# A two-layer decoder trunk: the first gain row spread by TensorE, the turn between layers summed by transfers, and transposes moved behind gate tiles

## The reference

```python
xn = rmsnorm(h, pre_g[i])
y = mixer_i(xn)                     # xn @ w_in, mixing over tokens, then @ w_out
h = h + rmsnorm(y, post_g[i])
gate = sigmoid(rmsnorm(h, ple_g[i]) @ w_ple_gate[i])
h = h + gate * (p[i] @ w_ple[i])
# rmsnorm: x * rsqrt(mean(x*x) + EPS) * g, one mean per token
```

## Time and profile before

| what | value |
|---|---|
| median of 3 runs | 1005.5 us (1005.45 to 1008.51) |
| the profiled execution, time | 1008.02 us |
| its span, first to last instruction | 1006.2 us |
| PE busy | 978.7 us (97%) |
| DVE busy | 642.7 us (64%) |
| ACT busy | 507.4 us (50%) |
| POOL busy | 91.7 us (9%) |
| moved by transfers | 150.37 MB, mean 149 GB/s |

### The profile page before, as it was taken

How to read it: one execution, slowest core, us unless ns; L and a number is a source line. 1 busy time by engine, 2 the same in 40 slices (tenths; PEclk the granted TensorE clock), 3 DMA queues, 4 the chain that set the end, 5 groups by cost and what they waited for, 6 DMA issues and landing times.

```text
span 1006.2 us, 12025 instructions
## 1 busy us (share of the span) xinstructions
PE 978.7 (97%) x4486; PEld 803.1 (80%) x4486; DVE 642.7 (64%) x863; ACT 507.4 (50%) x832; POOL 91.7 (9%) x148
## 2 busy tenths in 40 slices
PE   6999999999999999998989999999999999999998
PEld 4888888888877888786778888888888888888776
DVE  5767788786874225658886856776576676421835
ACT  6454545555562233546546647465654775341722
POOL 2020110100000003103000011010101000000500
PEclk9999999999999999999989999999999999999999
DMA  9555946848361523422938465573839063242122
GB/s 360 184 147 147 276 140 171 213 164 209 65 207 42 216 84 105 168 84 87 229 145 209 125 168 138 155 180 113 222 124 239 12 170 135 92 160 84 45 81 84
DMA packets 24760, 150.37 MB, mean 149 GB/s; under 512 B 3072, under 2 KB 4224, under 8 KB 8448
## 3 DMA queue, kind: packets, MB, share of 16 engines
q1 hardware_dynamic: 18800, 106.63, 27.7%
q0 software_dynamic: 5904, 42.99, 22.1%
HBM read 145.42 MB, written 4.19 MB: 149 GB/s over the span
## 4 chain that ended last, share of the span: by engine, by line
PE 88%; DVE 5%; ACT 3%; issue 2%; POOL 2%; DMA 1%; POOLq 0%; DVEq 0%; ACTq 0%
PE bank L2035 17%; PE bank L2038 16%; PE bank L2037 16%; PE bank L1962 8%; PE bank L1963 8%; PE bank L1964 8%; PE bank L2059 2%; PE bank L2060 1%; PE bank L2061 1%; PE bank L2288 1%; DVE w_lo L1309 1%; ACT square L683 1%; PE bank L2270 1%; PE bank L2292 1%; DMA raw<-in_slots 1%
## 5 line engine op out<-in xcount | busy, mean ns | idle before, releaser
L1309 DVE TENSOR_TENSOR w_lo<-raw,w_hi 128x1024 fp32r<-128x1024 f32 x204 | 240.8, 1222 | 140.0 <-ACT w_hi L719 136.4
L2035 PE MATMUL bank<-w_hi,l_hi 128*128 128x512 f32 x784 | 318.2, 406 | 6.8 <-issue 4.3
L2038 PE MATMUL bank<-w_hi,l_lo 128*128 128x512 f32 x784 | 306.9, 392 | 0.0
L2037 PE MATMUL bank<-w_lo,l_hi 128*128 128x512 f32 x784 | 306.6, 391 | 0.0
L719 ACT ACTIVATE w_hi<-raw 128x1024 fp32r<-128x1024 f32 x204 | 204.4, 1053 | 84.7 <-PE bank L2038 50.6
L2035 PEld LDWEIGHTS bank<-w_hi,l_hi 128*128 128x128 f32 x784 | 148.0, 189 | 40.8 <-issue 10.3
L2038 PEld LDWEIGHTS bank<-w_hi,l_lo 128*128 128x128 f32 x784 | 147.9, 189 | 31.6
L2037 PEld LDWEIGHTS bank<-w_lo,l_hi 128*128 128x128 f32 x784 | 148.1, 189 | 30.3 <-issue 1.0
L1274 DVE TENSOR_TENSOR w_lo<-raw,w_hi 128x1024 fp32r<-128x1024 f32 x52 | 61.3, 1222 | 117.3 <-ACT w_hi L672 117.2
L672 ACT ACTIVATE w_hi<-raw 128x1024 fp32r<-128x1024 f32 x52 | 52.3, 1057 | 134.2 <-PE bank L1964 122.3
L1962 PE MATMUL bank<-w_hi,y_hi 128*128 128x512 f32 x224 | 90.6, 404 | 0.2 <-DVE y_lo_end L1487 0.2
(11 more groups left out here) (221 smaller groups left out, 1190.2 us busy)
## 6 DMA issues: line engine op xcount, KB each, us to landing
raw<-in_slots SPq DMA_DIRECT2D x86, 1024.0 KB, 6.5
raw<-in_slots POOLq DMA_DIRECT2D x41, 1024.0 KB, 8.4
h<-in_x SPq DMA_DIRECT2D x8, 512.0 KB, 5.9
out<-h SPq DMA_DIRECT2D x4, 512.0 KB, 4.3
h<-out SPq DMA_DIRECT2D x4, 512.0 KB, 7.0
out<-h SPq DMA_DIRECT2D x8, 256.0 KB, 2.0
p_sb<-in_p SPq DMA_DIRECT2D x2, 512.0 KB, 3.8
g_post<-in_g_rows SPq DMA_DIRECT2D x2, 512.0 KB, 5.7
```

The lines of the kernel that those rows point to most:

```text
L1309: dve.tensor_tensor(w7_lo[:, ring(g), c], raw7[:, source(*STEPS[g]), c], w7_hi[:, ring(g), c].bitcast(F32), ALU.subtract).then_inc(w7_lo_r ...
L2035: pe.matmul(dst[:, :], left_hi, w7_hi[:, r, c], start=(first and k == 0), stop=False, skip_group_check=True)
L2037: pe.matmul(dst[:, :], left_hi, w7_lo[:, r, c], start=False, stop=False, skip_group_check=True)
L2038: done = pe.matmul(dst[:, :], left_lo, w7_hi[:, r, c], start=False, stop=(k == 3), skip_group_check=True)
```

## The change

Four things are changed.

**Start.** The gain row goes to one partition, and PE spreads it over the others with two matmuls against a row of ones; DVE copies the result out of PSUM. Unit 0's first block arrives in two halves, each with its semaphore, and is split half by half, with the left operand's parts in between. The two wide warming matmuls become 11 and 6 small ones.

**Norms.** ACT's squares are scaled so that they sum to the mean, and POOL's `rstd_of` has two operations instead of three, in all 24 norms of this kind.

**Tails.** The last tile's transposes (`transpose_x(l, 3)`) follow the gate's first token tile in both layers. The second layer's first transposes (`first_transpose(1, 0)`) follow the whole gate.

**Turn.** Unit 7's sums of weights are made by four adding transfers (into BV, twice into BX, into BA) in place of DVE's four half-block additions and one adding transfer; B12 is loaded twice for it. Buffer names change with it, for unit 7 and the even units behind it. ACT, DVE and POOL have another order of work from the second half of the gate to the end of unit 7.

```diff
 def x_buffer(u):
-    return BX if u % 2 else BV
+    return BX if u % 2 else BV if u < LEAD else BA
+def a_buffer(u):
+    return BA if u < LEAD else BV
+def s6_count(u):
+    return 2 * (u - (u >= LEAD))
...
+        sp.dma_start(scaled[0:1, 1], g_rows[0:1, :]).then_inc(g_in, 16)
         sp.dma_start(h[:, 0], x[0:P, :]).then_inc(x_in[0], 16)
-        row(g_first, g_rows[0:1, :], g_in)
         sp.dma_start(h[:, 1], x[P:2 * P, :]).then_inc(x_in[1], 16)
-        block_in(0, B11, BX, x_raw_in)
+        for half in range(2):
+            c = slice(half * SLOT // 2, (half + 1) * SLOT // 2)
+            sp.dma_start(raw7[:, BX, c], slots[B11][:, c]).then_inc(w_first[half], 16)
...
-        block_in(FIRST[1], B12, BV, v_raw_in)
+        block_in(FIRST[1], B12, BV, a_in)
...
         sp.wait_ge(gated_ready, 8)
+        block_in(FIRST[1], B12, BA, v_raw_in)
         for t in range(TILES):
             sp.dma_start(out[t * P:(t + 1) * P, :], h[:, t]).then_inc(h_out, 16)
...
             pool.wait_ge(ready, count)
-            link(pool.tensor_tensor(dst, first, second, ALU.add))
-            link(pool.tensor_scalar(dst, dst, 1.0 / D, EPS, ALU.mult, ALU.add))
+            link(pool.tensor_scalar(dst, first, second, EPS, ALU.add, ALU.add))
...
         tail_norms(0)
+        pool.wait_ge(a_in, 16 * LEAD)
+        add_in(LEAD, B11, BV, added_in[5])
+        pool.wait_ge(w7_lo_ready, split_done(LEAD, 1))
+        add_in(LEAD, B12, BX, s6_added)
         for t in range(TILES):
             pre(4 + t)
+        pool.wait_ge(s6_added, 16)
+        add_in(LEAD, B22, BX, s6_added)
...
-        pool.wait_ge(s5_sum, 2)
-        add_in(FIRST[1], B22, BV, added_in[7])
+        pool.wait_ge(v_raw_in, 32)
+        add_in(LEAD, B22, BA, added_in[7])
...
@@ ACT, start
-        hi7(0)
-        first_left(0)
+        first_high(0)
+        first_left(0, (0,))
+        first_high(1)
+        first_left(0, (1,))
+        first_left(1)
         x_squares(2)
-        first_left(1)
         first_full(0)
@@ ACT, gate of layer 0
+            tanh(1, 3)
             if l == 0:
                 left(1, 0, 0, 1, 11)
+                next_norm(2, 1)
                 left(1, 0, 1, 2, 12)
-            tanh(1, 3)
-            if l == 0:
-                next_norm(2, 1)
+                next_norm(3, 1)
                 left(1, 1, 0, 1, 11)
                 left(1, 1, 1, 2, 12)
-                next_norm(3, 1)
                 hi7(TURN + 1)
+                left(1, 2, 0, None, 21)
+                left(1, 2, 1, 4, None)
+                b_copy(LEAD, 0)
+                left(1, 3, 0, None, 21)
+                left(1, 3, 1, 4, None)
+                b_copy(LEAD, 1)
@@ DVE, unit 7, all of it after the change
+        left_7(1)
+        left_sum(1, 5)
+        lo7(TURN + 2)
+        left_6(1)
+        lo7(TURN + 3)
+        left_sum(1, 6)
+        left_3(1)
+        left_sum(1, 7)
+        left_sum(1, 3)
+        lo7(TURN + 4)
+        lo7(TURN + 5)
+        c_make(7, 0)
+        c_make(7, 1)
+        lo7(TURN + 6)
+        gate_rows()
+        lo7(TURN + 7)
+        s5_make(7, 0)
+        s5_make(7, 1)
+        gate_sums()
+        lo7(TURN + 8)
+        s6_add(8)
+        gate_maxima(0)
+        gate_maxima(1)
@@ PE, start
+        for half in range(2):
+            pe.matmul(bank[half][:, :], mask[0:1, :], scaled[0:1, 1, half * SEQ:(half + 1) * SEQ], start=True,
+                      stop=True).then_inc(g_spread, 1)
+        warming(11)
         first_transpose(0, 0)
-        for tp in range(2):
-            done = pe.matmul(b_of(tp)[:, :], ident[:, :], h[:, 0, 0:SEQ], start=True, stop=True)
-        done.then_inc(warm, 1)
+        warming(6).then_inc(warm, 1)
@@ PE, tail
-            transpose_x(l, 3)
...
-                        if l == 0 and nb == 1 and q == 1 and t == 2:
-                            first_transpose(1, 0)
+                        if q == 0 and nb == 0 and t == 0:
+                            transpose_x(l, 3)
...
         tail(0)
+        first_transpose(1, 0)
         first_transpose(1, 1)
         product(7, 1, 0)
```

160 lines of the change are left out of this document (72 added, 88 removed).

## The result

The changed kernel takes 995.95 us (median of 4 runs, 995.63 to 996.68) where the kernel before takes 1005.88 (4 runs, 1005.45 to 1008.51); the ratio is 0.9898, with an interval of 0.9883 to 0.9914. The forecast was 991.7, so the direction was right and the measured time 4.2 us above it: outside the forecast's own range (989.5 to 993), inside the outer one (988.5 to 996.5). The profiled execution took 995.63 us (span 993.6), against 1008.02 for that of before: 12.4 us between the profiles, 9.9 between the medians. The sum was made against the profile, so it is compared with the profile: 16.3 promised, 12.4 delivered.

What follows compares the result with a forecast made beforehand. PE, 97% busy, was taken as the bound, losing time only at four places. Start 1.75, first tail 4.0, turn 7.95, second tail 2.6 sum to 16.3: 1008.0 - 16.3 = 991.7 us; range 989.5 to 993, outer 988.5 to 996.5.

Steps and rivals of the forecast that it cites:

- the four places: Start, first tail, turn and second tail hold what PE lacks; all the rest is PE at its pace, untouched.
- Start: Kernel start: first block lands earlier, first product at 12.3, product 21 near 20; 1.75 us saved, bounds 0.5 and 2.6.
- the small warming: Rival at the start: low clock in first products, or halves landing together; 1.25 us lost, 993.0; chance 0.06.
- 0.4 us in each tail: Both tails: one norm operation less on POOL shortens PE's wait for `gated` by 0.3 to 0.4 us, taken as 0.4.
- Transposes behind the gate's first tile: Both tails: the gate's first tile fills the 1.84 us wait; 3.6 us saved in the first, 2.2 in the second.
- Gate's end, with a new wait of 2.75 us: Gate's end: PE stands still 2.75 us after the first transposes, yet product 2 starts at 471.3; 1.05 us saved.
- Unit 7: Turn: DVE loses four half additions, product 4 starts at 506.4, 6.7 us earlier, without the low clock; 6.9 us more saved.
- The prediction is wrong if a transfer is named ahead of ACT's split of block 6 or of unit 8's first: Sign at the turn: neither of these two splits on ACT should wait for its transfer.
- the rival of late transfers: Rival at the turn: transfers land late, costing 3.0 us and 3.0 of low clock, 997.7; chance 0.12.
- The rival with 0.19: Rival at the gate's end: the new 2.75 us wait lowers the clock, 1.7 to 3.0 us, 993.4 to 994.7; chance 0.19.
- I do not subtract the 2.5 us again: Baseline: sum made against the profile's 1008.0; the median's 2.5 us less read as low clock that goes with the change.

Runs made afterwards that it cites:

- old_start: The changed kernel with the start of the kernel before (gain row broadcast by its transfer, first block in one piece, two wide warming matmuls): 995.01 us, ratio 0.9885.
- decay_behind: The kernel before, only that ACT takes log_decay behind its split of unit 8's first block: 1006.59 us, ratio 1.0003.

## Why the prediction was right, and where it failed

The measured time lies inside the stated range only by its outer end, which was there for the clock and for the bounds of start and transfers. The direction, and the mechanism of three of the four places, were right; the start went the other way, below even its own lower bound of 0.5 us saved. That the range held is in part luck: the start's error used up room that was meant for other risks.

**What bounds the kernel**: right. The four places held everything; between them PE ran at its pace in both profiles.

**Start: the step that failed is the chain from ACT's start "at 8.2 instead of 10.41" to "the first product starts at 12.3"**. ACT did start early, at 7.87, even before I had it. But the sum went from engine to engine and never laid PE's own row of work out in time. The diff has 11 matmuls ahead of the first transposes; I named them as "the small warming" in a rival and gave their own time no price. PE's pace at its start was in the trace of before: its first eight transposes took 1.94 us (8.66), where such a group takes 1.04 later. Eleven warming matmuls at that pace are the 4.85 us measured, and the first product started at 14.43. Taking six of them away brought 1.67 us at product 21, of the 2.6 that the term was off. The rest is in the chain behind: 20.05 was forecast for product 21, and the runs without that hold reach 20.9 while the fourth `scaled` stands ahead of `w_lo`; without warming this `scaled` began at 18.32 and not at 17.6.

**Norms: "0.4 us in each tail"**. The second tail gave 0.5, the first took 0.1, together half of the forecast. The mechanism (POOL's operations stretched by DVE's) was right, but its sign does not follow from it: the phase between two engines decides which operation is hit. In `old_start`, with the same two operations, the first tail's wait of 0.42 us went whole, as forecast.

**Transposes behind the gate's first tile**: right in mechanism and size, 3.69 and 2.14 us against 3.6 and 2.2, and alone worth 5.5 us of the median.

**Gate's end, with a new wait of 2.75 us**: right, 2.65. Product 2 came 0.97 us earlier, forecast 1.05.

**Unit 7**: product 4 was forecast at 506.4; with the 2.56 us by which the profile after is ahead at 456.25, this is 503.84, and it started at 504.75. Of the 0.9 us 0.57 are the wait for unit 8's first block, which landed at 500.5 and not by 499.4 (502 less that shift); the rest had built up before (product 5 at 474.79, forecast 474.5). The wait at the row transposes was 0.56, forecast 0.8.

**"The prediction is wrong if a transfer is named ahead of ACT's split of block 6 or of unit 8's first"**: by this sign of my own it is wrong about the transfers. One is named ahead of both, for 0.82 and 1.13 us. Operand 6's second adding transfer was issued at 463.05 and landed at 474.86, 11.8 us later, where 9.6 were counted; only the slack behind it hid this. Unit 8's first block took 11.7 us from 488.84, where 11 were counted. So the rival of late transfers came true, with 0.57 us at PE of the 6 that it was priced at. The Trainium skill's fit (DMA: Bandwidth & Descriptors, Anatomy of one DMA) gave an estimate of 4.4 us for 1 MB. POOL's transfers took 11.8 us in the median at the turn and 9.0 over the whole kernel, so the measured times decide.

**The clock.** The rival with 0.19 was half right. In the profile after the wait of 2.65 us did not lower the clock, but of the seven profiles of kernels that have it, at 2.65 or 2.66, four show the fall and three do not. It is one chance of about two per execution, at 1.3 to 1.6 us, and not one outcome for the kernel. The same reading corrects the last point:

**The baseline: "I do not subtract the 2.5 us again"**. The profile of before was an execution with the low clock in both of its places. In the profile of `decay_behind` the wait of 1.84 us at 413.24 was the same and the transposes behind it took 1.17 us, not 1.76: no fall. The runs of the kernel before agree: of 34 that were taken beside the experiments, the ten with a granted clock of 0.997 or more took 1004.6 to 1006.2 us, the 14 with 0.994 or less, as the profile of before had, 1007.3 to 1009.6. Had I subtracted from a typical execution, with a part of the 1.7 and 3.0 us in it, the sum would have been smaller; the medians differ by 9.9 us and the profiles by 12.4. The forecast for the changed kernel itself is not hurt by this, since its own profile (995.63) is near its median.

So of the 4.2 us by which the forecast missed, 2.6 are the start, 0.7 the first tail's norm and what little the first layer added, 0.7 the turn with the gate's end, and 0.3 the difference of profile and median; the tails give 0.2 back, and what lies behind the last landmark and around the span was 0.1 longer.

What stays open: why PE's pace doubles at 10.6 in some starts and past 12 in others (nothing in the program differs there), and half of what the three-operation norm costs. The turn's sums were not taken back by themselves in any run: that its 7.3 us come from the four adding transfers and the new order of DVE is read from the landmarks and the waits that went, and is not split between them. Nor does a run show how much of the late landing of unit 8's first block is the work of the extra transfers, for in the kernel before it took 10.8 us too (498.06 to 508.87).
